# The second mixer's convolution: ScalarE scales 24 taps into a ring of three, GpSimd only adds them, VectorE keeps seven

## The reference, cut to what matters

```python
for l in range(DEPTH):
    h = rms_norm(x, norm_mix_g[l])
    p = h @ w_in[l]
    y_a = conformer_conv(p[..., :CONV_CH], p[..., CONV_CH:o1],
                         conv_w[l], conv_b[l], conv_ln_g[l], conv_ln_b[l])
    ...   # y_b: block attention with 4 heads; y_c: gated linear attention with 4 heads
    y = concatenate([y_a, y_b, y_c]) @ w_out[l]
    x = x + y
```

## Time and profile before

| | before |
|---|---|
| median of three runs | 2270.57 us |
| the profiled execution | 2271.53 us |
| its span | 2269.7 us |
| PE, PEld busy | 2225.0, 1957.8 us |
| DVE, ACT, POOL busy | 1738.7, 1335.7, 217.3 us |
| mixer of layer 0 in the second block | about 1631 to 1752 us |
| mixer of layer 1 | about 1950 to 2068 us |

### The profile page before, as it was taken

How to read it: one execution, slowest core, us unless ns; L and a number is a source line. 1 busy time by engine, 2 the same in 40 slices (tenths; PEclk the granted TensorE clock), 3 DMA queues, 4 the chain that set the end, 5 groups by cost and what they waited for, 6 DMA issues and landing times.

```text
span 2269.7 us, 35176 instructions
## 1 busy us (share of the span) xinstructions
PE 2225.0 (98%) x13623; PEld 1957.8 (86%) x13623; DVE 1738.7 (77%) x1748; ACT 1335.7 (59%) x1234; POOL 217.3 (10%) x189
## 2 busy tenths in 40 slices
PE   8999999999999999999999999999998999999998
PEld 8999999999888888888788888888897999888997
DVE  5557544656788888888888888888787777798776
ACT  5643434464477777677767777777555444545443
POOL 2000000100000000000000000000193000590000
PEclk9999999999999999999999999999999999999999
DMA  9444655634599999999999999999733555534551
GB/s 295 140 147 152 205 183 185 182 112 136 180 346 360 364 346 374 348 370 344 359 350 369 351 359 361 348 373 345 229 123 111 186 184 178 160 112 159 184 191 50
DMA packets 307912, 559.09 MB, mean 246 GB/s; under 512 B 10066, under 2 KB 145988, under 8 KB 307824
## 3 DMA queue, kind: packets, MB, share of 16 engines
q1 hardware_dynamic: 302784, 544.85, 69.2%
q0 software_dynamic: 5040, 13.03, 1.9%
HBM read 555.74 MB, written 2.11 MB: 246 GB/s over the span
## 4 chain that ended last, share of the span: by engine, by line
PE 84%; POOL 4%; ACT 3%; DVE 3%; POOLq 2%; DMA 1%; issue 1%; DVEq 0%; ACTq 0%
PE ps L656 26%; PE ps L658 26%; PE ps L657 26%; POOLq L637 2%; POOL agT L638 2%; POOL tap L632 2%; ACT w_hi L1416 1%; DMA xr<-x_rows,token_of 1%; PE ps L1097 1%; DVE w_lo L1850 1%; PE ps L723 1%; PE ps L707 1%; PE ps L870 0%; PE ps L1150 0%; PE ps L1080 0%
## 5 line engine op out<-in xcount | busy, mean ns | idle before, releaser
L1850 DVE TENSOR_TENSOR w_lo<-raw,w_hi 128x2048 fp32r<-128x2048 f32 x518 | 1184.1, 2295 | 312.0 <-ACT w_hi L1416 309.6
L1416 ACT ACTIVATE w_hi<-raw 128x2048 fp32r<-128x2048 f32 x518 | 985.6, 1908 | 340.9 <-PE ps L658 332.2
L656 PE MATMUL ps<-xT_hi,w_hi 128*128 128x256 f32 (+1 forms) x1712 | 488.7, 285 | 8.2 <-DVE xT_lo L1881 5.1
L657 PE MATMUL ps<-xT_lo,w_hi 128*128 128x256 f32 (+1 forms) x1712 | 484.1, 283 | 0.0
L658 PE MATMUL ps<-xT_hi,w_lo 128*128 128x256 f32 (+1 forms) x1712 | 484.1, 283 | 0.0
L656 PE MATMUL ps<-w_hi,xg_hi 128*128 128x512 f32 x896 | 360.2, 402 | 0.0
L658 PE MATMUL ps<-w_hi,xg_lo 128*128 128x512 f32 x896 | 354.0, 395 | 0.0
L657 PE MATMUL ps<-w_lo,xg_hi 128*128 128x512 f32 x896 | 353.7, 395 | 0.0
L656 PEld LDWEIGHTS ps<-xT_hi,w_hi 128*128 128x128 f32 (+1 forms) x1712 | 326.4, 191 | 13.9 <-issue 7.4
L657 PEld LDWEIGHTS ps<-xT_lo,w_hi 128*128 128x128 f32 (+1 forms) x1712 | 326.6, 191 | 1.5
L658 PEld LDWEIGHTS ps<-xT_hi,w_lo 128*128 128x128 f32 (+1 forms) x1712 | 326.5, 191 | 0.4
(11 more groups left out here) (470 smaller groups left out, 2678.3 us busy)
## 6 DMA issues: line engine op xcount, KB each, us to landing
raw<-in_exp_w SPq DMA_DIRECT2D x336, 1024.0 KB, 6.7
raw<-in_ffn_w_up SPq DMA_DIRECT2D x44, 1024.0 KB, 5.1
raw<-in_w_in SPq DMA_DIRECT2D x41, 1024.0 KB, 6.1
raw<-in_ffn_w SPq DMA_DIRECT2D x33, 1024.0 KB, 5.1
raw<-in_ffn_w_down SPq DMA_DIRECT2D x22, 1024.0 KB, 5.4
raw<-in_w_gate SPq DMA_DIRECT2D x16, 1024.0 KB, 5.6
raw<-in_w_out SPq DMA_DIRECT2D x8, 1024.0 KB, 4.9
raw<-in_w_o SPq DMA_DIRECT2D x6, 1024.0 KB, 5.4
```

The lines of the kernel that those rows point to most:

```text
L656: pe.matmul(out, lhs[0], rhs[0], start=first, stop=False)
L657: pe.matmul(out, lhs[0], rhs[1], start=False, stop=False)
L1416: act.activation(w_hi[:, u.const % SPL, 0:width], raw[:, u.const % RAW, 0:width], ACT.Copy)\
L1850: dve.tensor_tensor(w_lo[:, u.const % SPL, 0:width], raw[:, u.const % RAW, 0:width], w_hi[:, u.const % SPL, 0:width].bitcast(F32), ALU.sub ...
```

## The change: what it does

ScalarE takes over the scaling of taps 0 to 23, in eight groups of three placed among its other work (`taps(0)` to `taps(7)`), two `activation` Copies of 128x256 with a per-partition scale for each tap, into a ring of three slots, `scaled`. GpSimd waits for each tap (`tap_scaled`) and adds it (`tap_added`), 23 additions. ScalarE waits for the addition three taps back before it overwrites a slot. VectorE keeps taps 24 to 30: four where it had four before, two behind `ahead(5)`, one behind `ahead(6)`; the pieces behind `ahead(7)` and `gated(0)` are gone. The join moves from behind `gated(1)` to directly behind `gated(0)`, and the centring moves ahead of `low(yM_lo[:, 2:4, :], ...)`.

```diff
-POOL_TAPS = range(0, 18)
+SUMMED_TAPS = 24
+TAP_RING = 3
@@ GpSimd @@
-                pool.wait_ge(S_.glu_ready, L + 1)
-                pool.wait_ge(S_.p2_cols_ready, L + 1)
-                def tap(k, dst):
-                    for c in range(2):
-                        pool.tensor_scalar(dst[:, c, :], avT[:, c, k:k + S], cols2[:, 2 * k + c:2 * k + c + 1], None, ALU.mult)
-
-                tap(POOL_TAPS[0], conv_part)
-                tap(POOL_TAPS[1], tap2[:, 1])
-                for k in POOL_TAPS[1:]:
-                    pool.drain()
-                    m = pool.tensor_tensor(conv_part[:], conv_part[:], tap2[:, k % 2], ALU.add)
-                    if k + 1 in POOL_TAPS:
-                        tap(k + 1, tap2[:, (k + 1) % 2])
-                m.then_inc(S_.conv_part_ready, 1)
+                for k in range(1, SUMMED_TAPS):
+                    pool.wait_ge(S_.tap_scaled, L * SUMMED_TAPS + k + 1)
+                    if k > 1:
+                        pool.drain()
+                    pool.tensor_tensor(conv_part[:], conv_part[:] if k > 1 else scaled[:, 0], scaled[:, k % TAP_RING], ALU.add)\
+                        .then_inc(S_.tap_added, 1)
@@ ScalarE @@
+                def taps(n):
+                    for k in range(3 * n, 3 * n + 3):
+                        if k >= TAP_RING:
+                            act.wait_ge(S_.tap_added, L * (SUMMED_TAPS - 1) + max(k - TAP_RING, 1))
+                        for c in range(2):
+                            m = act.activation(scaled[:, k % TAP_RING, c, :], avT[:, c, k:k + S], ACT.Copy,
+                                               scale=cols2[:, 2 * k + c:2 * k + c + 1])
+                        m.then_inc(S_.tap_scaled, 1)
...
                 out(2, qcT[:], bank(0, 2, S), scale=float(GDK) ** -0.5)
+                act.drain()
+                act.wait_ge(S_.glu_ready, L + 1)
+                taps(0)
                 ahead(3)
...
                 ahead(4)
+                taps(1)
...
                 ahead(5)
+                taps(2)
...
                 ahead(6)
+                taps(3)
                 out(6, qbT[:], bank(0, 2, S))
                 ahead(7)
+                taps(4)
                 out(7, kbT[:], bank(1, 2, S))
                 ahead(8)
+                taps(5)
...
                 ahead(9)
+                taps(6)
                 out(9, rt2[:, :, 0:256], bank(1, TT, 256), ACT.Silu)
...
                 pT_pair(0)
+                taps(7)
                 square_root(S_.sqrt2_in, S_.sqrt2_out, L * 3 + 1, stat[:, 96:104])
@@ VectorE @@
                 ahead(7)
-                convolve(2)
...
                 gated(0)
-                convolve(2)
+                dve.wait_ge(S_.tap_added, (L + 1) * (SUMMED_TAPS - 1))
+                dve.tensor_tensor(cvT[:], cvT[:], conv_part[:], ALU.add).then_inc(S_.conv_ready, 1)
                 low(yM_lo[:, 0:2, :], 7, 70, yM_hi[:, 0:2, :], 1)
-                convolve(CW - taps[0])
                 ahead(10)
                 gated(1)
-                dve.wait_ge(S_.conv_part_ready, L + 1)
-                dve.tensor_tensor(cvT[:], cvT[:], conv_part[:], ALU.add).then_inc(S_.conv_ready, 1)
...
                 dve.tensor_scalar(col(112, 8), col(112, 8), RMS_EPS, None, ALU.add).then_inc(S_.sqrt2_in, 1)
+                dve.wait_ge(S_.channel_psum, L * 2 + 1)
+                for c in range(2):
+                    m = dve.scalar_tensor_tensor(cvT[:, c, :], ps[:, 7, 0:S], -1.0 / S, cvT[:, c, :], ALU.mult, ALU.add)
+                m.then_inc(S_.cent_ready, 1)
                 low(yM_lo[:, 2:4, :], 3, 72, yM_hi[:, 2:4, :], 2)
```

More of the change, by code:

```diff
@@ L229, in build @@
         with ExitStack() as shared:
-            tap2 = sb("tap2", [P, 2, 2, S], scope=shared)
+            scaled = sb("scaled", [P, TAP_RING, 2, S], scope=shared)
             dg = sb("dg", [P, TT, P], scope=shared)
@@ L2377, in mixer2 @@
                 x_parts(L * 8 + 24, 4, scale=gain(2 * L))
-                taps = [POOL_TAPS[-1] + 1]
+                taps = [SUMMED_TAPS]
                 def ahead(n):
@@ L2387, in convolve @@
                             w = cols2[:, 2 * k + c:2 * k + c + 1]
-                            if k == POOL_TAPS[-1] + 1:
+                            if k == SUMMED_TAPS:
                                 dve.tensor_scalar(cvT[:, c, :], avT[:, c, k:k + S], w, cols2[:, 62 + c:63 + c], ALU.mult, ALU.add)
@@ L2553, in mixer2 @@
                 m.then_inc(S_.yb_ready, 1)
[L2554 to L2557, removed]
                 ahead(11)
```

## The result

Eight runs of the changed kernel have a median of 2276.17 us (2274.61 to 2281.13), eight of the kernel before 2270.59 (2269.01 to 2271.61): ratio 1.0028, 95% interval 1.0017 to 1.0039. The change costs 5.6 us. The forecast was 2265.9, with 2271.5 as its upper end.

The account below looks back on a forecast made before the run. TensorE, 98% busy, bounds the kernel, so only its waits and low clock can be won. Layer 0 -4.7, layer 1 -1.4, one new clock fall +1.4: -4.7 us, forecast 2265.9, range 2261.5 to 2271.5.

Parts of the forecast that it names:

- The tail: TensorE's wait for the join before the channel sums goes: layer 0 gains 7.3 us with the clock, layer 1 0.4.
- The taps: ScalarE's scaling Copies: 0.404 us start to start, 2.4 us per group of three, 19.4 us per layer.
- The gate chain: taps(0) and taps(1) delay the transposes of within_chunks: TensorE stands 2.0 us in layer 0, 1.7 in layer 1.
- The square root: taps(7) ahead of it: wait before the gated transposes 1.4 us against 0.80 in layer 0, 1.35 against 2.36 in layer 1.
- the exclusion of the two engines: VectorE with two SBUF inputs and GpSimd reading SBUF block each other; additions meeting VectorE take 3.0 + 0.15 us.
- The clock: Old falls go, -2.25 us in layer 0's tail and -1.4 in layer 1; one new fall at new standstills, +1.4.
- The sum again: Forecast sum: layer 0 -4.7 us, layer 1 -1.4, one new fall +1.4, total -4.7; chance 0.37.
- no fall of the clock: Case in which the new standstills of TensorE do not lower its clock: 2264.5 us, chance 0.23.
- The additions set the pace: Rival: most additions meet VectorE, the 23rd ends 4.2 us after TensorE wants the sum: 2278.8 us, chance 0.10.
- Dearer taps: Rival: taps of 0.55 us, 0.88 more per group at three exposed places per layer: 2272.6 us, chance 0.14.

Follow-up runs that it names:

- experiment 1: The changed kernel with VectorE's three later taps moved from around ahead(5) and ahead(6) to behind ahead(8): 2262.32 us, ratio 0.9965 to the kernel before.

## Why the prediction was wrong, step by step

**The tail, right.** No wait before the channel sums in either layer. The join was over at 1719.9, 7 us before TensorE's channel sums.

**The taps, right.** 2.50 us per group, 0.40 apart.

**The gate chain, mechanism right, size too large.** 1.26 and 1.25 us instead of 2.0 and 1.7. In layer 0 the Exp behind `taps(1)` began at 1667.81, 2.6 us later than before and not 3.1. **The square root, right:** 1.39 and 1.37 us instead of 1.4 and 1.35.

**The failed step** is the sentence that closes the gate chain: "The split for T(6), the state steps and the scores hang on the same instruction of DVE and shift with TensorE." They did not shift with TensorE; it stood for them 1.40 + 2.68 us in layer 0 and 1.42 + 2.69 in layer 1. The price that was left out is GpSimd's on VectorE. The prediction priced the exclusion of the two engines only on GpSimd's side (additions of 3.0 us beside a split; measured 3.12 to 3.15). It had the other side in its rows: L2461 took 1.82 us instead of 0.7 because GpSimd held it off, and a split 3.25 instead of 2.3. But it gave VectorE's later taps and the copies no such term, and took it that fewer GpSimd instructions mean less in VectorE's way. What counts is how densely the additions lie: one per 5.37 us before, one per 1.45 us after. Six short instructions took 7.74 us, and 2.79 undisturbed (experiment 1).

Step by step against the kernel before, in layer 0: VectorE's state steps end at 1696.05 instead of 1689.20, 6.85 us later, 1.31 of them by the gate chain. Of the other 5.54 the taps are 4.55 (7.74 against 2.10 + 1.09) and the copies 1.88 (2.66 against 0.78), while one split got 0.85 shorter. TensorE had 1.0 us of room there, so it came 4.5 us later, 4.08 of them as waits. Layer 1 comes to the same waits by another sum: there the taps had been dear already, so they add only 2.3 us (7.74 against 3.29 + 2.13), the copies 0.9 and two splits 1.0, and TensorE had no room.

The Trainium skill (SBUF — State Buffer, "Who interferes with whom") says that whoever issues first holds the shared ports for the whole instruction and that issue order decides who blocks. For the additions the runs agree: a split stretches one addition by 1.9 us, but a short instruction of VectorE waits out an addition of 1.29 us. For GpSimd's scalings, which read SBUF too, the exclusion that the prediction took from there is seen on one side only: a split held one off (3.97 us for two instead of 1.82), but four taps beside them took 2.10 us, 1.82 undisturbed.

**The clock, half right.** The forecast had one new fall and the 2.36 us wait's fall gone. The profile has the new one, behind 2.69 us, in layer 1, and both old ones are gone. But over the runs the account leaves the changed kernel as much beside its waits as before (2261.7 and 2261.0), and four of the eight runs have a mean clock of 0.993 or 0.994 where the profiled one has 0.995: the gain of -2.25 and -1.4 is not seen in the median.

**The sum again.** Layer 0: -4.7 forecast, +4.1 new waits, -0.7 gate chain: -1.3; measured -1.1. Layer 1: -1.4 forecast, +4.1 new waits, +1.5 for the low clock (from L1269 to the second pair of transposed probabilities 17.78 us instead of 16.26 in layer 0), -0.5 gate chain: +3.7, measured +3.6. Without the new waits and the falls the forecast's mechanism holds: its case "no fall of the clock" was 2264.5, and with the gate chain's measured sizes 2263.3; experiment 1 measured 2262.3. This sum is of the profiled execution, whose span of 2272.3 us is the shortest of the eight (up to 2279.1). The medians lie 5.6 apart: 4.5 are the waits (14.5 against 10.0), and the remaining 1.1 go beside them, so the gain by the clock that the profile shows isn't there in the others. What the clock did in those runs is known by its mean alone.

**The rivals.** "The additions set the pace" named the right pair of engines and the wrong victim: the additions had 7 us to spare, and VectorE's own work paid. At 1.55 us mean they were far from the 2.97 at which that rival decides. "Dearer taps" is refuted by 0.40 us. Its time, 2272.6, was nearer the result by chance.

## What to carry to other kernels

When work is moved off GpSimd, look at what its remaining instructions then lie beside. A dense row of additions on GpSimd made five of six short VectorE instructions with two inputs in SBUF wait one out, so put VectorE's short ones where GpSimd is idle, and price the collision on both sides. When TensorE is 98% busy, add up its waits per kernel: a wait that is taken away is won in full unless another chain ends within the same distance, and which chain that is has to be read from the timeline before the next move. Here the kernels with a wait of 2.4 us or more lost 4 to 5 us beside their waits, and those with none over 1.7 did not.

## What the runs showed of the hardware that was not expected

Copies of 128x128 from SBUF to SBUF on VectorE, with one input each, were held up as well: four in 2.66 us beside additions, in 0.64 without. The twelve state steps, which take one of their inputs from PSUM, were not: 4.00 us beside additions, 4.01 before. Two scalings of 128x256 on GpSimd beside the two-input taps cost these almost nothing: 2.10 us for four, 1.82 undisturbed. And the same wait of 2.7 us before the same instruction lowered the clock in one layer and not in the other, within one execution.
